# Three-branch prompt attention: the second head's turned probabilities copied by VectorE instead of ScalarE

## The reference, cut to what matters

```python
def gqa_attend(q, k, v, qpos, kpos, mask, slopes):
    s = jnp.einsum('...qgrd,...kgd->...grqk', q, k) * NSA_SCALE
    s = s - slopes[:, :, None, None] * dist
    p = masked_softmax(s, mask)
    return jnp.einsum('...grqk,...kgd->...qgrd', p, v), p
...
o = gate[:, :, 0] * o_cmp + gate[:, :, 1] * o_sel + gate[:, :, 2] * o_win
```

## Time and profile before

| | |
|---|---|
| median of 3 runs | 3036.32 us (3026.58 to 3043.79) |
| the profiled execution | 3032.79 us, its span 3031.0 us |
| TensorE busy | 2640.0 us, 87% of the span |
| VectorE busy | 1139.6 us, 38% |
| ScalarE busy | 870.4 us, 29% |
| GpSimd busy | 142.3 us, 5% |
| the copies, L2573 | 384 instructions, 158.8 us, mean 463 ns |
| the transposes, L2490 | 1056 instructions, 161.5 us busy |
| the bias passes, L2630 | 103.0 us busy in the shapes without a carried maximum |

### The profile page before, as it was taken

The page is one execution under the profiler, slowest core; times in us unless marked ns, Lnnn a source line. Parts: engine busy times, 40 slices in busy tenths (PEclk is TensorE's granted clock), DMA queues, the critical chain, the costliest instruction groups (busy, mean ns, idle before and its releaser), DMA issues. The chain is left out here.

```text
span 3031.0 us, 68839 instructions
## 1 busy us (share of the span) xinstructions
PE 2640.0 (87%) x25240; PEld 1726.3 (57%) x25240; DVE 1139.6 (38%) x3238; ACT 870.4 (29%) x2098; POOL 142.3 (5%) x233
## 2 busy tenths in 40 slices
PE   6999888899995559799998799979999997888878
PEld 4556455666663534345546687966666665554534
DVE  3111345545544931101100000035656554666633
ACT  1111344433332110010100000036767664443400
POOL 0000000011110100000000000000000001222100
PEclk9999899999997679899997899989999998899989
DMA  4000200177775141431006476630000004767732
GB/s 178 23 15 13 68 1 1 33 221 227 225 227 87 17 149 56 141 125 50 35 31 180 152 226 218 198 141 2 2 2 2 2 2 124 223 216 214 235 113 75
DMA packets 312602, 322.12 MB, mean 106 GB/s; under 512 B 72283, under 2 KB 289547, under 8 KB 311820
## 3 DMA queue, kind: packets, MB, share of 16 engines
q1 hardware_dynamic: 225980, 234.78, 25.0%
q10 hardware_dynamic: 86288, 82.94, 9.0%
HBM read 290.57 MB, written 30.27 MB: 106 GB/s over the span
## 5 line engine op out<-in xcount | busy, mean ns | idle before, releaser
L2200 PE MATMUL bank<-cm_room 64*64 64x114 f32 (+1 forms) x4608 | 296.8, 441 | 5.3 <-DMA cm_room<-cache_nsa_kv 5.2
L2200 PEld LDWEIGHTS bank<-cm_room 64*64 64x64 f32 x4608 | 252.9, 162 | 46.2 <-DMA cm_room<-cache_nsa_kv 6.1
L2020 PE MATMUL bank<-cm_room 128*128 128x512 f32 (+3 forms) x576 | 225.0, 551 | 0.0
L2573 ACT ACTIVATE np_pT<-bank 128x512 f32<-128x512 f32 (+3 forms) x384 | 158.8, 463 | 143.5 <-PE bank L2490 143.3
L2564 ACT ACTIVATE np_p<-np_p,np_nmax 128x640 f32<-128x640 f32 (+7 forms) x256 | 187.2, 735 | 5.4 <-DVE np_coef L2638 5.1
L2490 PE MATMUL bank<-ident,np_p 128*128 128x128 f32 x1056 | 161.5, 285 | 24.8 <-ACT np_pT L2573 19.1
L313 PE MATMUL bank<-ev_hT,ev_w 128*128 128x384 f32 (+1 forms) x576 | 176.8, 467 | 6.1 <-ACT zaT L256 6.1
L2504 PEld LDWEIGHTS bank<-kv,np_pT 128*64 128x64 f32 x4224 | 133.5, 138 | 77.0 <-ACT np_pT L2573 50.5
L2630 DVE CUSTOM_DVE_ANT_0 np_p<-bank,np_tab 128x128 f32<-128x128 f32 (+3 forms) x256 | 103.0, 439 | 195.6 <-issue 115.7
L2020 PEld LDWEIGHTS bank<-cm_room 128*128 128x128 f32 (+1 forms) x576 | 103.9, 182 | 117.3 <-issue 106.4
L2481 PE MATMUL bank<-kT,np_q 64*128 64x512 f32 (+3 forms) x768 | 161.6, 509 | 5.1 <-DVE np_nmax L2630 3.9
(11 more groups left out here) (513 smaller groups left out, 3809.7 us busy)
## 6 DMA issues: line engine op xcount, KB each, us to landing
ms_pg<-cache_mla SPq DMA_DIRECT2D x388, 144.0 KB, 2.9
ns_pg<-cache_nsa_kv SPq DMA_DIRECT2D x320, 128.0 KB, 2.9
cm_room<-cache_nsa_kv ACTq DMA_DIRECT2D x262, 128.0 KB, 3.8
cm_room<-cache_nsa_kv SPq DMA_DIRECT2D x250, 128.0 KB, 4.3
ns_pg<-cache_nsa_kv ACTq DMA_DIRECT2D x192, 128.0 KB, 3.2
ms_pg<-cache_mla ACTq DMA_DIRECT2D x124, 144.0 KB, 3.4
ev_w<-w_in_even SPq DMA_DIRECT2D x8, 768.0 KB, 10.3
cm_room<-w_in_odd SPq DMA_DIRECT2D x24, 256.0 KB, 7.0
```

What stands on the lines that cost most here:

```text
L2020: t = nc.tensor.matmul(bank[:n, f, 0:hi - lo], hT[:, i // 3 % 2, k, at:at + n], wt[:, k, lo:hi], start=k == 0, stop=k == KD - 1)
L2200: t = nc.tensor.matmul(out(blk)[kind * HD:(kind + 1) * HD], phi[blk * BLK:(blk + 1) * BLK, kind, x, :], rows(kind, blk, x), start=x == 0, ...
L2573: nc.scalar.activation(pT[:, g % NPT, :(hi - lo) * P], bank[:, f, :(hi - lo) * P], ACT.Copy).then_inc(S["evA"], 1)
```

## The change

ScalarE no longer copies the second head's chunks; VectorE does. `turned(*mine[0])` and `turned(*mine[2])` stay on ScalarE, `mine[1]` goes to VectorE at the head of its round, ahead of the bias passes of u+3, and `mine[3]`, the second head's tail where there is one, behind them and ahead of `finish(u - 1)`. The ring's list names the new engine. The function `turned` on VectorE is ScalarE's with `tensor_copy`; buffers, waits and TensorE's order stay the same.

```diff
--- before.py
+++ after.py
@@ -2435,7 +2435,7 @@
             cmp_fills(0, k)
         for u in range(n):
             for v, ci in turns(u):
-                order.append((("T", v, ci), "A"))
+                order.append((("T", v, ci), "AD"[v % 2]))
             quad, k = task(u)
             if quad is not None:
                 cmp_fills(quad, k)
@@ -2594,12 +2594,11 @@
                     exponent(v)
                 for u in range(n):
                     mine = turns(u)
-                    for v, ci in mine[:2]:
-                        turned(v, ci)
+                    turned(*mine[0])
                     if u + 2 < n:
                         exponent(2 * u + 4)
-                    for v, ci in mine[2:]:
-                        turned(v, ci)
+                    if len(mine) > 2:
+                        turned(*mine[2])
                     if u + 2 < n:
                         exponent(2 * u + 5)
                     quad, k = task(u)
@@ -2676,9 +2675,21 @@
                     cmp(0, k)
                 for u, x in begin:
                     biased(u, x)
+                def turned(v, ci):
+                    f = ring.full(dve, S, ("T", v, ci))
+                    g = place[v, ci]
+                    if g >= NPT:
+                        dve.wait_ge(S["pv"], g - NPT + 1)
+                    lo, hi = chunks(v)[ci]
+                    V.tensor_copy(pT[:, g % NPT, :(hi - lo) * P], bank[:, f, :(hi - lo) * P]).then_inc(S["evD"], 1)
+
                 for u in range(n):
+                    mine = turns(u)
+                    turned(*mine[1])
                     for w, x in ahead(u):
                         biased(w, x)
+                    if len(mine) > 2:
+                        turned(*mine[3])
                     if u >= 1:
                         finish(u - 1)
                     quad, k = task(u)
```

## The result

The changed kernel takes 3140.66 us (median of 4; 3134.48 to 3142.46) against 3040.06 (median of 4; 3026.58 to 3051.82): 1.033 times as long, 95% interval 1.028 to 1.038. Its profiled execution took 3140.72 us, 108 more than that of before; the stage accounts for 99 of these. What follows the stage takes 498.5 and 498.4 us.

A forecast was written before the change was run, and what follows sets the result against it. TensorE was taken as the bound, busy 474 of the stage's 508 us. Two-chunk rounds' 75 us plus narrow rounds' 5, together 80, on the profiled 3032.8 gave 3113, with part of a 3.5 offset 3115; range 3078 to 3150.

The forecast's parts named there:

- The bound and the sign: In the stage TensorE is the bound, and the change makes it wait for VectorE's tail copy: slower, chance 0.88.
- The loop's price: Tail turned, bias pass, tail copied, second head turned, scores: 3.18 us at five blocks against 2.17, plus 1.0 a round.
- the seven-block round: Two-chunk round, seven blocks here and seven ahead: 5.69 us from the tail's start against 4.18, plus 1.5.
- the late one: Last rounds of a run, four or three blocks ahead: 2.62 us from tail to scores against 1.78, plus 0.84 each.
- The sum: Over the stage's two-chunk and one-chunk rounds, 75 and 5 us of loss, together 80.
- the two-chunk rounds: 64 of 128 rounds, keys of five to eight blocks turned as first four blocks and a tail: 75 us lost.
- the narrow ones: One-chunk rounds of smallest width, VectorE back to back: about 0.21 us more per copy, 5 us in all.
- The signs named ahead: Stage near 588 us; TensorE waits over 60 times before L2490, 80 to 120 us; np_nmax waits nearly gone; 5.8 tail to tail.
- ScalarE's relief at nothing: Removing 192 of ScalarE's 384 copies gains nothing; TensorE's 19.1 us of waiting for its copies is not returned.
- The clock: Rival: TensorE's stands in two-chunk rounds lower its granted clock to 0.93, 36 us more, 3150; chance 0.12.
- The weighed rule: Copies from PSUM are slower on VectorE than ScalarE (658 against 570 ns for 512): 17 us at the very most.

The follow-up runs named there:

- e1: Changed kernel with VectorE's copy of the second head's tail moved ahead of the bias passes of u+3: 3063.1 us, 1.007 times the kernel before.
- e2: Changed kernel with only the second head's first chunks copied by VectorE, all tails back on ScalarE: 3047.4 us, 1.002 times the kernel before.
- e6: Changed kernel with eight buffers of np_p instead of six, the compressed bias table loaded per quad: 3026.4 us, 0.997 times the kernel before.
- e3: Changed kernel with only the second head's 64 tails copied by VectorE, all first chunks back on ScalarE: 3139.4 us, 1.033 times the kernel before.
- e4: Changed kernel with the heads swapped: VectorE copies the first head's chunks, ScalarE the second's: 3209.2 us, 1.055 times the kernel before.
- e5: Changed kernel with VectorE's copy of the second head's tail moved behind finish(u - 1) too: 3231.5 us, 1.064 times the kernel before.
- e11: Changed kernel with TensorE turning the tails of u ahead of the weighted sum of u-1: 3042.7 us, 1.001 times the kernel before.
- e10: Kernel before with only the tails of u turned ahead of the weighted sum of u-1, six buffers: 2994.8 us, 0.984 times the kernel before.

## Why the prediction was right

The forecast was 3115 us in a range of 3078 to 3150, and 3140.7 came.

- **The bound and the sign.** TensorE bounds the stage and its transposes would queue behind a copy that queues behind the bias pass: shown by the trace, and by e1, e2 and e6, which each take one link away and get most or all of the time back; e3 shows that the 64 tails alone make the whole loss.
- **The loop's price.** Tail to scores at five blocks: 3.18 was the sum, 3.25 is what the rows show (2368.63 to 2371.88). For the seven-block round I had 5.69 from tail to weighted sum, for the late one 2.62 from tail to scores. After, at full clock, 5.73 (2410.79 to 2416.52) and 2.68 (2470.94 to 2473.62):

```profile
2410.79 0.88 PE L2490 MATMUL bank<-ident,np_p 128*128 128x128 f32 x6
...
2416.52 1.85 PE L2504 MATMUL bank<-kv,np_pT 128*64 128x64 f32 x56
...
2470.94 0.44 PE L2490 MATMUL bank<-ident,np_p 128*128 128x128 f32 x2
...
2473.62 0.92 PE L2481 MATMUL bank<-kT,np_q 64*128 64x384 f32 x4
```

- **The sum.** 75 us for the two-chunk rounds and 5 for the narrow ones; measured 78 us more idle time in the stage. Idle time is a fair measure of the loop: in the 40 two-chunk rounds that ran at full clock in both profiles, the rounds (weighted sum to weighted sum) are 48.4 us longer and TensorE's idle time in them 48.7. The narrow rounds' 5 us were too many: the 62 other stretches, measured the same way, take 154.5 us before and 155.9 after, 1.4 more, and 154.4 in e3, whose VectorE has no first chunks to copy.
- **The signs named ahead.** TensorE waits 55 times for VectorE's copy before L2490, not over 60, 1.5 us each, 80.8 in all, the lower end of 80 to 120; the scores' wait for `np_nmax` went from 3.9 to 0.5 us; tail to tail at five blocks is 5.85 us, 5.8 was said. The stage is 607.5 us long, not near 588: the difference is the clock.
- **ScalarE's relief at nothing.** Right: 19.1 and 18.9 us.
- **The clock.** This is the term that I sized apart and did not take into the sum. I gave it a chance of 0.12 and 36 us. It came: TensorE's busy time rose by 21 us. 78 and 21 are the stage's 99 us; the forecast of 3115 lacked the second, and the result lies nearer to this rival's 3150. That the range held it is owed to the rival's figure, which was the range's upper end. The windows over the four runs of two-chunk rounds after:

```profile
2055.64:2169.63 113.99, 87.79 (x1098) 60.28 (x1096) 63.16 (x221) 46.42 (x101) 2.31 (x2) 0.93 0.01 2
2210.95:2326.21 115.26, 89.16 (x1099) 60.63 (x1097) 63.11 (x221) 46.42 (x101) 2.31 (x2) 0.91 0.01 1
2367.55:2479.90 112.35, 85.96 (x1098) 59.26 (x1096) 63.17 (x221) 46.41 (x101) 2.27 (x2) 0.94 0.01 2
2521.23:2624.30 103.07, 75.52 (x1027) 51.16 (x1025) 58.42 (x212) 44.69 (x98) 0.00 (x0) 0.98 0.01 2
```

Together that is a clock of 0.94, near the 0.93 that I had taken, and 27 us short of full speed. But the same four runs gave 0.98, 0.98, 0.98 and 1.00 before, 5 us short already, which my 36 did not take off. The chance was too low: the clock fell in each kernel that closed the loop, to 0.95 in e3, 0.90 in e4 and 0.88 in e5.

- **The weighed rule.** By the copies' own lengths at most 17 us were possible. The 128 long and short first copies of e2 on VectorE cost nothing that the times can tell, so the copies' lengths made no part of the loss that could be measured. The estimates of 658 and 570 ns, worked out from the table of the Trainium skill, VectorE: DVE Perf Modes, section on the TRN2 errata, lie below the 691 and 598 of the earlier trace rows by about 30 ns each. The clock swung in this trace, 0.58 granted in one round and 1.00 in the same kind of round 157 us later. That agrees with the Trainium skill, TensorE: Matmul & The Clock Gate, section on a second failure mode, psum-queue depth-cycling, which tells of a clock made to swing by short idle times between groups of matmuls (the section on thin matmuls has long waits for DMA).

## What to carry to other kernels

When a copy is moved to a less busy engine, what counts is not that engine's share of busy time but what stands ahead of the copy in its queue, and what that waits for: here a 0.28 us copy behind a 1.8 us pass closed a loop through TensorE and VectorE, and cost 78 us and, by the clock, some 20 more. A dependency that reuses a buffer of the very round that is being worked on is where this loop closed. Two more buffers opened it (e6); the producing step moved ahead of a long independent one left it closed but let that work run beside it (e11). If TensorE stands 0.35 us in each round for the same copy, look first at what it could do in the meantime: here the order of TensorE's own queue was worth 1.6%, and another engine for the copy gained nothing in any order that was run.

## What was not expected of the hardware

The clock's part grew faster than the waits. The same matmuls were busy for 474.0 us in the kernel before, 494.6 in the changed one, 519.9 in e4 and 540.4 in e5, at idle times of 34.5, 112.9, 161.6 and 162.6 us and granted clocks of 0.99, 0.96, 0.90 and 0.88. From before to after, 78 us of standing went with 21 of slower matmuls; from after to e5, 50 more went with another 46. And e4 and e5, equal in idle time, differ by 20 us in busy time. The sum of the waits doesn't order the clocks: e1, with 54.0 us idle, was granted 1.00, the kernel before with 34.5 only 0.99. The longest single wait orders them better: 0.86 us in e1, 2.2 in the changed kernel, 3.2 in e4 and 3.8 in e5. That is seen, not tested; no run parts the length of a wait from the sum.

Nor does TensorE have to stand for the clock to fall. In e10 it is busy without a gap for the 9 us up to 2093, the last 3.5 of them with the 32 narrow matmuls of the compressed scores (L2515), and then falls to the lower level:

```profile
2084.00:2093.00 9.00, 9.00 (x128) 7.77 (x125) 3.62 (x18) 5.14 (x11) 0.00 (x0) 1.00 0.01 2
2093.00:2096.50 3.50, 3.50 (x17) 2.40 (x18) 0.69 (x1) 1.85 (x4) 0.00 (x0) 0.52 0.00 0
```

All the rounds of the kernel before in which the clock falls are the three with these matmuls (0.85 in each). Which property the clock followed in all of these is left open.
